# B's blocks laid out by the host, C weighted in pieces, late transfers moved, and experts found by replacing: a hybrid S5, attention and mixture-of-experts block

## The reference, cut to what matters

```python
coef_r = ((abar_r - 1.0) * lr + abar_i * li) / den
coef_i = (abar_i * lr - (abar_r - 1.0) * li) / den
bbar_r = coef_r[..., None] * br - coef_i[..., None] * bi
bbar_i = coef_r[..., None] * bi + coef_i[..., None] * br
bu_r = jnp.einsum('bsgc,gpc->bsgp', uf, bbar_r)
bu_i = jnp.einsum('bsgc,gpc->bsgp', uf, bbar_i)
...                                  # x[t] = abar * x[t-1] + bu[t], complex
y = einsum('gcp,bsgp->bsgc', c_re, xr) - einsum('gcp,bsgp->bsgc', c_im, xi)
```

## Time and profile before

| what | value |
|---|---|
| runs | 1159.68 us median of 3 (1158.82 to 1162.73) |
| the profiled execution | 1159.92 us, of which the span from first to last instruction is 1158.0 us |
| PE, DVE, ACT, POOL busy | 97%, 38%, 12%, 9% of the span |
| granted TensorE clock | 0.998 of full speed |
| HBM traffic | 459.46 MB, mean 397 GB/s |

### The profile page before, as it was taken

The page is one execution under the profiler, slowest core; times in us unless marked ns, Lnnn a source line. Parts: engine busy times, 40 slices in busy tenths (PEclk is TensorE's granted clock), DMA queues, the critical chain, the costliest instruction groups (busy, mean ns, idle before and its releaser), DMA issues.

```text
span 1158.0 us, 17087 instructions
## 1 busy us (share of the span) xinstructions
PE 1122.6 (97%) x6970; PEld 491.0 (42%) x6970; DVE 442.8 (38%) x952; ACT 140.9 (12%) x313; POOL 105.1 (9%) x142
## 2 busy tenths in 40 slices
PE   8999999999999999999999999999999999999996
PEld 6657788544333333333333333333333333333332
DVE  7857668263222333332222322222222222222224
ACT  3222240231000000000000000000000000000002
POOL 6496810000000000000000000000000000000000
PEclk9999999999999999999999999999999999999999
DMA  9983389999999999999999999999999999999994
GB/s 385 393 305 102 101 335 400 421 349 422 423 427 434 428 428 430 431 430 430 430 434 429 429 432 430 431 425 431 431 430 431 430 431 432 431 431 426 427 424 202
DMA packets 39839, 459.46 MB, mean 397 GB/s; under 512 B 3732, under 2 KB 4248, under 8 KB 16120
## 3 DMA queue, kind: packets, MB, share of 16 engines
q1 hardware_dynamic: 39088, 458.09, 94.3%
q10 hardware_dynamic: 712, 0.81, 0.2%
HBM read 457.83 MB, written 1.05 MB: 396 GB/s over the span
## 4 chain that ended last, share of the span: by engine, by line
PE 78%; DMA 18%; DVE 1%; ACT 1%; issue 1%; SPq 1%; DVEq 0%
PE ps L1086 30%; PE ps L1133 17%; DMA ring<-in_w_gu 16%; PE ps L662 5%; PE ps L1054 4%; PE ps L998 3%; PE ps L847 2%; PE ps L659 2%; PE ps L1110 2%; PE ps L865 2%; DMA ring<-in_first 1%; PE ps L830 1%; PE ps L922 1%; PE ps L623 1%; PE ps L629 1%; PE ps L1118 1%
## 5 line engine op out<-in xcount | busy, mean ns | idle before, releaser
L1086 PE MATMUL ps<-ring,zone 128*64 128x512 f32 x1024 | 227.0, 595 | 9.6 <-DMA ring<-in_w_gu 9.6
L1133 PE MATMUL ps<-ring,tmp 128*64 128x512 f32 x1012 | 224.2, 594 | 10.4 <-ACT tmp L1363 10.4
L1086 PE MATMUL ps<-zone 128*64 128x512 f32 x1024 | 227.2, 595 | 1.3 <-DMA zone<-in_w_gu 1.2
L1854 DVE TENSOR_TENSOR x_tok<-x_tok,ps 128x512 f32<-128x512 f32 x128 | 81.9, 681 | 261.4 <-PE ps L1054 260.1
L1086 PEld LDWEIGHTS ps<-ring,zone 128*64 128x64 f32 x1024 | 70.7, 137 | 161.6 <-issue 143.5
L1133 PEld LDWEIGHTS ps<-ring,tmp 128*64 128x64 f32 x1012 | 83.2, 137 | 130.7 <-issue 130.7
L1086 PEld LDWEIGHTS ps<-zone 128*64 128x64 f32 x1024 | 70.7, 137 | 154.1 <-issue 146.9
L1360 ACT ACTIVATE tmp<-hT 128x256 f32<-128x256 f32 x64 | 23.9, 417 | 722.8 <-DVE hT L1869 722.8
L1869 DVE TENSOR_SCALAR hT<-ps 128x256 f32<-128x256 f32 x64 | 24.2, 419 | 189.9 <-PE ps L1086 189.9
L1848 DVE TENSOR_TENSOR tmp<-ps,zone 128x512 f32<-128x512 f32 x32 | 22.1, 691 | 162.8 <-PE ps L1133 162.8
L1054 PE MATMUL ps<-tmp,xn_tok 64*128 64x512 f32 x248 | 70.0, 641 | 0.0
(11 more groups left out here) (339 smaller groups left out, 889.5 us busy)
## 6 DMA issues: line engine op xcount, KB each, us to landing
ring<-in_w_down SPq DMA_DIRECT2D x60, 2048.0 KB, 17.8
zone<-in_w_gu SPq DMA_DIRECT2D x23, 4096.0 KB, 26.9
ring<-in_w_gu SPq DMA_DIRECT2D x23, 4096.0 KB, 29.2
zone<-in_w_gu SPq DMA_DIRECT2D x14, 2048.0 KB, 13.1
ring<-in_w_gu SPq DMA_DIRECT2D x13, 2048.0 KB, 14.1
ring<-in_w_ada SPq DMA_DIRECT2D x16, 1024.0 KB, 13.1
ring<-in_w_in SPq DMA_DIRECT2D x12, 1024.0 KB, 14.6
ring<-in_w_gu SPq DMA_DIRECT2D x10, 1024.0 KB, 9.5
```

Of the source, the lines that this page charges most:

```text
L1086: last = mm(ps[CAP * h:CAP * h + CAP, b, :], hg[:, 2 * j + kk, :], w[:, kk, D * b + 512 * h:D * b + 512 * h + 512], start=False, stop=(j = ...
L1133: last = mm(ps[CAP * h:CAP * h + CAP, 3, :], actT[:, q, j, :], row[:, 512 * h:512 * h + 512], start=False, stop=(j == DN_PIECES - 1 and q ...
L1854: V.tensor_tensor(x_tok[:, t, 512 * h:512 * h + 512], x_tok[:, t, 512 * h:512 * h + 512], ps[:, bank + h, :], ALU.add).then_inc(S["comb_ad ...
```

## The change

B is laid out by the host as it is used, without the coefficients: the array grows from 256 KB to 512 KB and goes straight into `BT`. `b_columns`, the mask products and the copy are gone. Since the recurrence is linear and diagonal, the coefficient may be applied behind it, and so C is multiplied by it, in four pieces on VectorE (`weighted_c(m)`), each ahead of the `largest` that follows an odd recurrence; the sign of the imaginary part is part of that. The products of B for the first two recurrences are issued together, into banks of their own (`BU_BANK`). ScalarE asks for the late transfers behind gelu and both sigmoids. `chosen` sets the lower four of the eight maxima to a very small number, replaces the first occurrence of each value in the padded logits by that number, and marks what has changed; one of the fills in front of it is gone.

```diff
 def b_layout(b_re, b_im):
-    return np.concatenate([b[0].reshape(ST, 2, N, C).transpose(1, 2, 0, 3).reshape(P, ST * C) for b in (b_re, b_im)], axis=1)
+    out = np.zeros((4, 2, C, 2, KW, 2, N), np.float32)
+    for r, w in enumerate((b_re, b_im)):
+        w = w[0].reshape(KW, 4, 2, N, C)
+        for q in range(2):
+            out[:, q, :, r, :, q, :] = w[:, :, q].transpose(1, 3, 0, 2)
+    return out.reshape(P, 2 * KW * P)
...
+    NONE = -3.0e38
+    BU_BANK = (4, 6, 4, 4, 4, 4, 4, 4)
...
-            sp.dma_start(b_in.rearrange("p r s c -> p (r s c)"), b_laid[:, :]).then_inc(S["const_in"], 16)
+            sp.dma_start(BT.rearrange("p r m n -> p (r m n)"), b_laid[:, :]).then_inc(S["const_in"], 16)
...
-            def b_u(j):
-                if j == 0:
+            def b_u(*pairs):
+                if pairs[0] == 0:
                     pe.wait_ge(S["proj_sb"], 1)
-                    pe.wait_ge(S["BT_sb"], 1)
+                    pe.wait_ge(S["const_in"], 48)
                 else:
-                    pe.wait_ge(S["scanned"], 4 * j)
+                    pe.wait_ge(S["scanned"], 4 * pairs[0])
                 for r in range(2):
-                    for q in range(2):
-                        s = 2 * j + q
-                        a = 32 * (s % 4)
-                        last = mm(ps[:, 4 + q, T * r:T * r + T], BT[a:a + 32, r, s // 4, :], uT[a:a + 32, s // 4, :],
-                                  start=True, stop=True, skip_group_check=True)
-                last.then_inc(S["bu_up"], 1)
+                    for j in pairs:
+                        for q in range(2):
+                            s = 2 * j + q
+                            a = 32 * (s % 4)
+                            last = mm(ps[:, BU_BANK[j] + q, T * r:T * r + T], BT[a:a + 32, r, s // 4, :], uT[a:a + 32, s // 4, :],
+                                      start=True, stop=True, skip_group_check=True)
+                last.then_inc(S["bu_up"], len(pairs))
...
             def c_x(m):
                 pe.wait_ge(S["xs_set"], 2 * m + 2)
-                if m == 0:
-                    pe.wait_ge(S["const_in"], 48)
-                    pe.wait_ge(S["c_set"], 1)
-                else:
+                pe.wait_ge(S["c_set"], 2 * m + 2)
+                if m > 0:
                     pe.wait_ge(S["y_skip"], m)
...
             proj(2, 0)
-            b_columns()
             turned_columns(0)
             proj(2, 1, (0,))
-            b_u(0)
+            b_u(0, 1)
             proj(2, 1, (1, 2, 3))
             proj(3, 0)
-            b_u(1)
             turned_columns(1)
...
             gate_up_biases()
-            fill(384), fill(384)
+            fill(384)
             pe.wait_ge(S["sel_set"], TT)
...
-            act.wait_ge(S["const_in"], 48)
-            nc.scalar.activation(CT[:, 1], CT[:, 1], ACT.Copy, scale=-1.0).then_inc(S["c_set"], 1)
-            ...                       # four masked copies into Bblk, the copy to BT
...                                     # the five act.dma_start move from here
             act.wait_ge(S["y_skip"], KW)
             nc.scalar.activation(gluT, uT, ACT.Gelu_apprx_tanh).then_inc(S["gelu"], 1)
             act.wait_ge(S["proj_sb"], 8)
             nc.scalar.activation(gbT, gbT, ACT.Sigmoid).then_inc(S["sig_gb"], 1)
             nc.scalar.activation(gaT, gaT, ACT.Sigmoid).then_inc(S["sig_ga"], 1)
...                                     # to here
-            ...                       # six products of b_in with the coefficients
+            def weighted_c(m):
+                if m == 0:
+                    dve.wait_ge(S["const_in"], 48)
+                cr, ci = (sprm[:, j, 4 * m:4 * m + 4].unsqueeze(2).to_broadcast([P, 4, 2 * C]) for j in (3, 4))
+                c0, c1 = (CT[:, r, m].rearrange("p (s c) -> p s c", s=4) for r in range(2))
+                t0, t1 = (tmp[:, r, 0:P].rearrange("p (s c) -> p s c", s=4) for r in range(2))
+                link(V.tensor_tensor(t0, c1, ci, ALU.mult))
+                link(V.tensor_tensor(t1, c0, ci, ALU.mult))
+                link(V.tensor_tensor(c0, c0, cr, ALU.mult))
+                link(V.tensor_tensor(c1, c1, cr, ALU.mult))
+                V.tensor_tensor(c0, c0, t0, ALU.subtract).then_inc(S["c_set"], 1)
+                V.scalar_tensor_tensor(c1, t1, -1.0, c1, ALU.mult, ALU.subtract).then_inc(S["c_set"], 1)
+                dve.wait_ge(S["c_set"], 2 * m + 2)
...
             recurrence(1)
+            weighted_c(0)
             for p in range(HEADS // 2):
                 largest(p)
...
                 if 2 * p + 3 < 8:
                     recurrence(2 * p + 3)
+                    weighted_c(p + 1)
...
                 link(V.max(top[:, i, :], lg[:, i, :]))
-                t4 = top[:, i, TOPK - 1:TOPK]
-                link(V.tensor_scalar(sel[:, i, :], lg[:, i, :], t4, None, ALU.is_gt))
-                link(V.tensor_reduce(rs[:, i, 1:2], sel[:, i, :], AX.X, ALU.add))
-                link(V.tensor_scalar(rs[:, i, 1:2], rs[:, i, 1:2], -1.0, float(TOPK), ALU.mult, ALU.add))
-                link(V.tensor_scalar(eq[:, i, :], lg[:, i, :], t4, None, ALU.is_equal))
-                link(V.tensor_tensor_scan(run[:, i, :], ones[:, 0:EXPERTS], eq[:, i, :], 0.0, ALU.mult, ALU.add))
-                link(V.scalar_tensor_tensor(eq[:, i, :], run[:, i, :], rs[:, i, 1:2], eq[:, i, :], ALU.is_le, ALU.mult))
-                V.tensor_tensor(sel[:, i, :], sel[:, i, :], eq[:, i, :], ALU.add).then_inc(S["sel_set"], 1)
+                link(V.memset(top[:, i, TOPK:8], NONE))
+                link(V.match_replace(unchosen[:, i, :], top[:, i, :], padded[:, i, :], NONE))
+                V.tensor_tensor(sel[:, i, :], lg[:, i, :], unchosen[:, i, 0:EXPERTS], ALU.not_equal).then_inc(S["sel_set"], 1)
...
             expert_of(0)
+            link(V.memset(padded[:, :, EXPERTS:EXPERTS + PAD], NONE))
```

More of the change, by code:

```diff
@@ L219, in stored @@
         return slice(P * (2 * (k % RUN) + k // RUN), P * (2 * (k % RUN) + k // RUN) + P)
-    def b_sum(r):
-        return tmp[:, r, 0:T].rearrange("p (s c) -> p s c", s=ST)
-    b_in = kT.rearrange("p m t -> p (m t)")[:, 0:512].rearrange("p (r s c) -> p r s c", r=2, s=ST)
     work = gbT.rearrange("p m t -> p (m t)")[:, 0:10 * ST].rearrange("p (j s) -> p j s", s=ST)
@@ L229, in state @@
         return sprm[:, j, :] if j < 5 else work[:, j - 5, :]
-    blk = z.rearrange("p b r n -> p (b r n)")
-    Bblk = blk[:, 0:1024].rearrange("p (r s q c) -> p r s q c", r=2, s=ST, q=2)
     wide = 2048
@@ L256, in build @@
     wr = probs[:, 0:256].rearrange("p (k e) -> p k e", k=KD)
-    rt = probs[:, 256:640].rearrange("p (j i e) -> p j i e", j=6, i=TT)
-    lg = probs[:, 640:704].rearrange("p (i e) -> p i e", i=TT)
+    rt = probs[:, 256:512].rearrange("p (j i e) -> p j i e", j=4, i=TT)
+    PAD = 8 - TOPK
+    padded, unchosen = (probs[:, a:a + TT * (EXPERTS + PAD)].rearrange("p (i e) -> p i e", i=TT) for a in (512, 608))
+    lg = padded[:, :, 0:EXPERTS]
     brt = probs[:, 704:736]
@@ L279, in build @@
     shift_set = sem("shift_set")
-    names = """x_in const_in head_in late_in gfin_in out_stored ones_set cond_set sprm_sb Bblk_set
-        BT_up BT_sb c_set phases modrow_sb modT_up mod1_sb sq1 xn1 xT_up
+    names = """x_in const_in head_in late_in gfin_in out_stored ones_set cond_set sprm_sb c_set phases modrow_sb modT_up mod1_sb sq1 xn1 xT_up
         hD_sb hA_sb proj_sb bu_up scanned xs_set xs_read rotated turned_up turned_sb sc_up negmax expd probs
@@ L288, in build @@
         x_split scale1_set turn turned row_max sqsum2 lnD lnA lnP
-        cond_half u_up biased_scale ada_used Bsum_set mask_set phase_hi scale2_set hgl_up hgl_sb sums_set""".split()
+        cond_half u_up biased_scale ada_used mask_set phase_hi scale2_set hgl_up hgl_sb sums_set""".split()
     S = {n: sem(n) for n in names}
@@ L695, in c_x @@
                 last.then_inc(S["xs_read"], 1)
[L697 to L705, removed]
             def turned_columns(n):
@@ L1262, in _ @@
             projected(0, uT)
-            act.wait_ge(S["const_in"], 48)
-            nc.scalar.activation(CT[:, 1], CT[:, 1], ACT.Copy, scale=-1.0).then_inc(S["c_set"], 1)
[L1265 to L1269, removed]
             projected(1, q_tok)
-            act.wait_ge(S["BT_up"], 1)
-            nc.scalar.copy(BT[:, :, :, :].rearrange("p r m n -> p (r m n)"), ps[:, 6:8, :].rearrange("p b n -> p (b n)")).then_inc(S["BT_sb"], 1)
             turned(0)
@@ L1283, in _ @@
             projected(7, gbT[:, 4:8, :])
+            act.wait_ge(S["y_skip"], KW)
+            nc.scalar.activation(gluT, uT, ACT.Gelu_apprx_tanh).then_inc(S["gelu"], 1)
+            act.wait_ge(S["proj_sb"], 8)
+            nc.scalar.activation(gbT, gbT, ACT.Sigmoid).then_inc(S["sig_gb"], 1)
+            nc.scalar.activation(gaT, gaT, ACT.Sigmoid).then_inc(S["sig_ga"], 1)
             act.dma_start(wr.rearrange("p (a b) e -> p a (b e)", b=RUN), w_router[0].rearrange("(a p b) e -> p a (b e)", p=P, b=RUN)).then_inc(S["late_in"], 16)
@@ L1288, in _ @@
```

(11 more changed lines are left out.)

## The result

| | before | changed |
|---|---|---|
| median of 20 runs each | 1160.08 us (1158.56 to 1162.73) | 1161.97 us (1160.11 to 1165.7) |
| ratio to before | | 1.0015, 95% interval 1.0009 to 1.0021 |
| profiled execution, span | 1159.92, 1158.0 us | 1161.88, 1160.1 us |
| mean granted TensorE clock | 0.998 | 0.996 |

The change costs 1.9 us, 0.15%. With 20 runs each the interval leaves out 1, so the kernel is slower, though by less than the 0.3% that the prediction took as the least that can be told. It forecast 1166.0 us, 6 us slower; the time lies inside its range and near its rival (a), 1162.6 us.

A forecast was written before the change was run, and what follows sets the result against it. Transfers set the end, counted from expert 0's start, and TensorE sets the pace before it. From 1159.9 us, 7.0 for the C pieces less 0.7 for the choice of experts gave 1166.2, stated as 1166.0, range 1160.5 to 1168.5.

The forecast's parts named there:

- rival (a): Each C piece's last operation slips in with the fifth: piece 6.5 us, cycle 21.9, TensorE 3.4 late, 1162.6 us; chance 0.26.
- What bounds the kernel: Transfers set the end, counted from when expert 0 starts to free its buffers; before that TensorE sets the pace.
- Part 1: B laid out by the host: TensorE saves 0.87 us of transposes and 0.6 by merged products, about 1.5 us ahead.
- Part 2: C weighted in four pieces on VectorE: operations with both operands in SBUF wait for GpSimd; TensorE 7.0 us late.
- A piece costs 0.9 + 5 x 1.35 = 7.7 us: VectorE's piece of C: each of six operations costs one GpSimd period of 1.35 us; bounds 1.95 and 9.9.
- with 7.7 it needs 23.05: VectorE's cycle, 15.4 us without a piece, becomes the bound over TensorE's 19.9, 3.15 us a cycle.
- 0.7 + 2 x 3.15 = 7.0 us late: TensorE behind the loop: first maximum 0.7 us later, then two full cycles each 3.15 us longer.
- Part 3: Late weights asked for behind gelu on ScalarE: gelu 2.4 us earlier, requests about 8 us later, effect on time 0.
- Part 4: Finding the experts, second token half: VectorE gains 0.93 us, one fill goes, TensorE 0.7 us earlier, 0.5 at least.
- The sum: Whole kernel: 1159.9 + 7.0 - 0.7 = 1166.2 us, given as 1166.0 against the median.
- a change beyond 0.3% for the worse: Whole kernel slower by more than 3.5 us, the least that can be told from none; chance 0.67.

The follow-up runs named there:

- experiment 1: Changed kernel with one wait more per piece of C, so that the last operation waits for the fifth (the waited version): 1167.12 us, ratio 1.0054.
- experiment 2: Changed kernel with one operand of each operation of the C pieces in PSUM, seven operations instead of six: 1157.92 us, ratio 0.9976.
- experiment 4: Changed kernel with TensorE's three idle gaps filled by 12 unused products of 128 x 128 each: 1168.78 us, ratio 1.0065.
- experiment 8: Kernel before the change with four more TensorE fills ahead of the position sums, holding up expert 0: 1162.52 us, ratio 1.0022.
- experiment 3: Changed kernel with each piece's six operations in three pairs, the second of a pair not waiting for the first: 1158.37 us, ratio 0.9984.
- experiment 9: Kernel before the change with only the five late transfers moved behind gelu and both sigmoids: 1160.53 us, ratio 1.0001.
- experiment 7: Kernel before the change with only the new choice of experts and one fill less: 1160.01 us, ratio 1.0002.
- experiment 5: Changed kernel with TensorE's three idle gaps filled by 5 unused products of 128 x 128 each: 1161.15 us, ratio 1.0010.
- experiment 6: Changed kernel with the old choice of experts and the late transfers back ahead of gelu: 1162.78 us, ratio 1.0027.

## Why the prediction was right or wrong

**What bounds the kernel: right.** The end moved with expert 0 (experiments 1, 2, 4 and 8).

**Part 1: right, the merged products undersized.** Sixteen instructions take 1.15 us where eight take 1.13: the merging is worth 1.06 us up to the next work, not 0.6. In experiment 2, where nothing eats it, TensorE reaches the last products with B at 132.15, 1.3 us earlier than before, and that execution's start-up was 0.7 late (44.51 against 43.78 at the same projection): 2.0 us. The Trainium skill's figure for four row tiles ("TensorE: Matmul & The Clock Gate", the table with small-K matmuls), from which the prediction had 1.2 us, was the better guide; the trace now has the 1.15.

**Part 2: the mechanism right, and the step that failed is "A piece costs 0.9 + 5 x 1.35 = 7.7 us", and with it "with 7.7 it needs 23.05".** Six operations were charged with a wait for GpSimd. Only five are: a piece costs 6.5 us. The argument for six was that GpSimd asks while the fifth operation still runs; experiments 1 and 3 show that this doesn't count, and that the operation queued directly behind on VectorE goes first, each time. A second term was too large as well: the 7.88 us from the maximum to the end of the scan held the wait of the small operation on the maxima, 0.66 us. Behind a piece that operation starts when GpSimd's instruction is all but over and takes 0.17 us, in the changed kernel and in experiment 1; the 7.88 became 7.4. The cycle is therefore 21.3 us, not 23.05, and below the 21.9 of rival (a) too.

The forecast had TensorE 0.7 + 2 x 3.15 = 7.0 us late behind the loop. Measured it is -0.64 + 2 x 1.46 = 2.28 us. Of the 4.7 us between, some 3.5 are the piece, charged 1.2 us too much three times, and 1.2 the small operation.

Experiment 1 is the prediction's own case, with six operations that wait, and took 1167.1 us against the 1166.0 forecast. That nearness is partly luck: its cycle was 22.45 us, not 23.05, and half clock made up the difference. Rival (a), 1162.6 us, is near the changed kernel's 1162.0 by luck too: it had TensorE 3.4 us late by waits alone, where 2.28 are waits and 1.7, in the profiled execution, the clock.

**The clock: not foreseen.** 1.7 us of the changed kernel's 3.97 at that place come from it in the profiled execution. The prediction put this term at nothing: it turned TensorE's idle time into its own length only. Over the 20 runs of the changed kernel the mean clock orders the times only in part (median 1164.4 us at 0.995, 1161.9 at 0.996, 1162.1 at 0.997, and the two runs above have 1160.1 and 1162.5), so what the clock costs in the median is open.

**Part 3: right in its 0**, with two wrong sizes on the way (experiment 9).

**Part 4: right.** 0.7 us forecast; 0.69 to 0.87 in the traces of experiments 7, 2 and 5. The replacement costs 0.3 us with its value load, where 0.4 was taken.

**The sum** with the measured terms: 1159.9 + 2.3 + 1.7 - 0.7 = 1163.2, and the profiled execution took 1161.88; most of what lies between is the expert stage, 1.0 us shorter in this execution. For the medians this doesn't serve: the terms give 3.3 us (1.6 without the clock), the medians differ by 1.9, and nothing here tells what makes the difference. Chances: rival (a) had 0.26, the forecast 0.50, and a change beyond 0.3% for the worse 0.67; it came out within 0.3%. What divided rival (a) from the forecast was a few hundredths of a microsecond of issue time; giving one side of it half of all chance was too sure, and a time between the two, 1164, would have been nearer.

## What to carry to other kernels

Before you put work into an engine's idle time, look at what the neighbour that shares its SBUF access does in that stretch: here an operation of VectorE with both operands in SBUF cost one whole instruction of a busy GpSimd, 1.3 us instead of 0.3. Put one operand in PSUM, or queue independent operations directly behind each other without a wait, so that several go in at one gap. And when you price a short idle gap of TensorE, look at the granted clock behind it: in one execution here 1.7 us of half clock followed three gaps of 1.2 to 1.4 us, in another with the same gaps nothing did.

## What the runs showed of the hardware

- A VectorE operation of 128 x 128 with two operands in SBUF and a wait before it ends 0.15 us behind GpSimd's current instruction, in every piece of the change. The next one of VectorE, if it waits for nothing, takes 0.28 us and holds GpSimd for 0.13 us (1.40 against 1.27). With a wait between them it takes 1.31 us. The Trainium skill, "SBUF — State Buffer" (Who interferes with whom), has the loser blocked for the whole instruction, which the 1.31 us bear out, and issue order deciding; to this the runs add that VectorE's next operation, if nothing makes it wait, goes ahead of GpSimd's next instruction (experiment 3, three times a piece).
- An operation of four elements with its one operand in SBUF is held too: L1607 ends at 107.42, 0.03 us behind GpSimd's instruction, after 0.66 us. Started just before such an end it takes 0.17 us (107.99).
- TensorE's clock fell from 2.4 to 1.2 GHz for about 3.4 us, 1.6 us behind the end of the third idle gap of the changed kernel's loop, and in the waited version 1.0 us behind the first and 0.5 us behind the third. The two profiles with the gaps filled show no fall in the loop; one with the gaps has none either (experiment 6). What decides is open.
- Falls of the same length are also elsewhere. In experiments 3 and 4 there is one at 9.4 and 9.7 us, at the end of a wait of TensorE for its first weights of 2.37 and 2.35 us, and the first products with B come 1.5 and 1.75 us later than in the changed kernel; in the other ten profiles the same wait is 0.6 to 1.8 us, and no fall follows. In experiment 2 there is one at 1136.9 us, behind idle times of only 0.3 us. Of 31 runs of the kernel before, those with a mean clock of 0.998 and more have a median of 1159.8 us and five with 0.996 one of 1161.6.
